# Ten split-operand buffers of a two-layer transformer kernel, set 32 to 224 bytes apart in SBUF

## The reference

```python
x = x + jnp.square(jax.nn.relu(hm @ w_up[l])) @ w_down[l]
...
hid = jax.nn.silu(xn @ w_gate[e]) * (xn @ w_up[e])
out = out + (hid * cw[..., e:e + 1]) @ w_down[e]
```

## Time and profile before

| | us |
|---|---|
| median of three runs | 964.89 |
| lowest and highest | 963.74, 967.37 |
| the profiled execution, its own time | 964.85 |
| its span, first to last instruction | 963.0 |
| TensorE busy | 947.5 |
| VectorE busy | 534.4 |
| ScalarE busy | 470.1 |

### The profile page before, as it was taken

The page is one execution under the profiler, slowest core; times in us unless marked ns, Lnnn a source line. Parts: engine busy times, 40 slices in busy tenths (PEclk is TensorE's granted clock), DMA queues, the critical chain, the costliest instruction groups (busy, mean ns, idle before and its releaser), DMA issues.

```text
span 963.0 us, 13218 instructions
## 1 busy us (share of the span) xinstructions
PE 947.5 (98%) x5313; PEld 722.7 (75%) x5313; DVE 534.4 (55%) x848; ACT 470.1 (49%) x733; POOL 2.5 (0%) x12
## 2 busy tenths in 40 slices
PE   9999999999999999999999999999999999999995
PEld 8878887887889998999889887889874354545432
DVE  5888896775666556555586874676453212122113
ACT  5488665756444444544566756445553121212113
POOL 0000000000000000000000000000000000000000
PEclk9999999999999999999999999999999999999999
DMA  9945465424455554554545725476858999999994
GB/s 314 303 143 173 155 238 179 156 107 163 152 189 190 204 175 175 175 181 156 202 150 175 246 104 175 131 259 223 290 205 286 393 394 393 394 393 395 393 396 157
DMA packets 107266, 223.49 MB, mean 232 GB/s; under 512 B 10186, under 2 KB 15043, under 8 KB 107203
## 3 DMA queue, kind: packets, MB, share of 16 engines
q1 hardware_dynamic: 104752, 219.10, 64.2%
q10 hardware_dynamic: 2450, 3.51, 1.1%
HBM read 221.54 MB, written 1.05 MB: 231 GB/s over the span
## 4 chain that ended last, share of the span: by engine, by line
PE 83%; DVE 7%; ACT 4%; issue 3%; DMA 2%; SPq 1%; POOL 0%; ACTq 0%; DVEq 0%; POOLq 0%
PE pb L477 17%; PE pb L479 17%; PE pb L478 17%; PE pb L2488 11%; PE pb L2511 5%; PE pb L2526 3%; PE pb L2455 2%; DVE wl L1552 2%; ACT wh L1003 2%; PE pb L567 2%; DMA BT<-in_w_exp_down 1%; PE pb L638 1%; DMA raw<-in_w_in 1%; PE pb L650 1%; PE pb L714 1%
## 5 line engine op out<-in xcount | busy, mean ns | idle before, releaser
L1552 DVE TENSOR_TENSOR wl<-raw,wh 128x2048 fp32r<-128x2048 f32 (+3 forms) x112 | 246.4, 2208 | 95.1 <-ACT wh L1003 94.8
L1003 ACT ACTIVATE wh<-raw 128x2048 fp32r<-128x2048 f32 (+3 forms) x112 | 206.7, 1852 | 108.6 <-PE pb L479 98.9
L477 PE MATMUL pb<-wh,th 128*128 128x512 f32 (+2 forms) x620 | 245.9, 397 | 0.2 <-DVE wl L1552 0.2
L479 PE MATMUL pb<-wh,tl 128*128 128x512 f32 (+2 forms) x620 | 239.0, 385 | 0.0
L478 PE MATMUL pb<-wl,th 128*128 128x512 f32 (+2 forms) x620 | 238.8, 385 | 0.0
L477 PE MATMUL pb<-th,wh 128*128 128x256 f32 x528 | 152.6, 289 | 0.0
L478 PE MATMUL pb<-tl,wh 128*128 128x256 f32 x528 | 149.4, 283 | 0.0
L479 PE MATMUL pb<-th,wl 128*128 128x256 f32 x528 | 149.4, 283 | 0.0
L477 PEld LDWEIGHTS pb<-wh,th 128*128 128x128 f32 x620 | 116.6, 188 | 26.1 <-issue 4.1
L479 PEld LDWEIGHTS pb<-wh,tl 128*128 128x128 f32 x620 | 116.4, 188 | 23.3
L478 PEld LDWEIGHTS pb<-wl,th 128*128 128x128 f32 x620 | 116.7, 188 | 20.4
(11 more groups left out here) (408 smaller groups left out, 1074.5 us busy)
## 6 DMA issues: line engine op xcount, KB each, us to landing
raw<-in_w_in SPq DMA_DIRECT2D x31, 1024.0 KB, 5.2
raw<-in_w_up SPq DMA_DIRECT2D x16, 1024.0 KB, 5.5
raw<-in_w_down SPq DMA_DIRECT2D x16, 1024.0 KB, 4.8
raw<-in_w_exp_gate SPq DMA_DIRECT2D x18, 512.0 KB, 11.2
raw<-in_w_exp_up SPq DMA_DIRECT2D x18, 512.0 KB, 11.9
raw<-in_w_xkv SPq DMA_DIRECT2D x8, 1024.0 KB, 5.1
raw<-in_w_exp_down SPq DMA_DIRECT2D x7, 1024.0 KB, 12.9
S<-in_w_exp_down SPq DMA_DIRECT2D x6, 1024.0 KB, 13.5
```

What stands on the lines that cost most here:

```text
L477: PE.matmul(o, lh, rh, start=start, stop=False, skip_group_check=True)
L479: return PE.matmul(o, ll, rh, start=False, stop=stop, skip_group_check=True)
L1003: ACTE.activation(hi_of(i), raw_of(i), ACT.Copy).then_inc(S["hi"], 1)
L1552: DVE.tensor_tensor(lo_of(i), raw_of(i), hi_of(i).bitcast(F), ALU.subtract).then_inc(S["lo"], 1)
```

## The change

Lines 193 to 196 get a small helper, `apart`, that declares an unused tensor of some fp32 columns ahead of a buffer. With 4 bytes a column the gaps are 32 bytes before tl0, wh0 and th1, 64 bytes before wh1, wh2, wl0, wl1 and wl2, 224 bytes before tl1, and none before th0. Sizes, names and uses of the buffers stay as they are, and the gaps are given back with the scope `early`.

```diff
--- before.py
+++ after.py
@@ -190,10 +190,19 @@
         RC = sb("RC", 2048)
         RDK = sb("RDK", 2048)
         RD, KT = RDK[:, 0:1024], RDK[:, 1024:2048]
-        TH, TL = [sbe("th0", 2048, R), 0], [sbe("tl0", 2048, R), 0]
-        WH = [sbe(f"wh{i}", SLOT, R) for i in range(NW)]
-        WL = [sbe(f"wl{i}", SLOT, R) for i in range(NW)]
-        TH[1], TL[1] = sbe("th1", 2048, R), sbe("tl1", 2048, R)
+        TH, TL, WH, WL = [0, 0], [0, 0], [0] * NW, [0] * NW
+
+        def apart(name, n, cols):
+            if cols:
+                sbe(f"gap_{name}", cols)
+            return sbe(name, n, R)
+
+        TH[0], TL[0] = apart("th0", 2048, 0), apart("tl0", 2048, 8)
+        for i in range(NW):
+            WH[i] = apart(f"wh{i}", SLOT, 8 if i == 0 else 16)
+        for i in range(NW):
+            WL[i] = apart(f"wl{i}", SLOT, 16)
+        TH[1], TL[1] = apart("th1", 2048, 8), apart("tl1", 2048, 56)
         BD = BT[:, 0:1024]
         TMP = BT[:, 1024:2304]
         PB = [ctx.enter_context(nc.psum_tensor(f"pb{i}", [128, 512], F)) for i in range(8)]
```

## The result

The changed kernel takes 969.25 us (median of 8 runs, 968.44 to 969.92) against 964.72 us of the kernel before in the same session (8 runs, 963.72 to 967.37). The ratio is 1.0045 with a 95% interval of 1.0034 to 1.0056: slower by 4.5 us. That is inside the 0.5% that I took as the least that can be told, but the interval leaves "no change" out, and the time lies above the range of 961 to 969. The profiled execution took 969.49 us, its span 967.6 us against 963.0.

A forecast was written before the change was run, and what follows sets the result against it. TensorE, busy 98% of the span, was taken to bound the kernel through the start-to-start time of three-pass matmuls. All terms were 0 us, summing to 0 against 964.85 us; forecast 964.9 us, range 961 to 969.

The forecast's parts named there:

- three-pass matmuls: 3,444 matmuls on lines 477 to 479: 0 us from moving their operands; range ends -13.3 and +7.5 ns each.
- The 288-column units: Line 477 at distances of 128, 256 and 384 bytes: 0.133 us per matmul at each, so distance gives nothing back.
- overhead of 13.3 ns: Width-independent remainder of each three-pass matmul; over 3,444 matmuls 45.9 us, the most the change could bring.
- The plain matmuls: Lines 541, 714 and 737, operands 0, 128 and 32 bytes apart: 0.216 us each, so distance gives nothing back.
- Line 2526: 512-column fp32r matmul, operands 160 bytes apart: 0.235 us, not less than 0.2275; distance gives nothing back.
- expert part: Stretch from 709.2 us on: same program at the same addresses, 0 us.
- B: Rival: new distances cost three-pass matmuls 7.5 ns each, 990.7 us, or 970 with one in five hit; chance 0.06.
- A: Rival: all 13.3 ns per three-pass matmul are same-distance collisions that end, 919.0 us, or 942 with half; chance 0.06.
- C: Rival: tl1 stays level with wh1, so if A holds those pairs keep their stall, 924 us; part of A's 0.06.
- The page's rule: Trainium skill page: loading the next tile's weights steals no read bandwidth from the running matmul; taken to speak against the change.
- ScalarE's and VectorE's splits: 112 splits on each engine, using the moved buffers: 0 us; at most 0.4 us per engine, covered by idle time.
- transfers: None writes the ten buffers while they are split operands; expert weights keep their addresses: 0 us.

The follow-up runs named there:

- e3: Kernel before the change, with only the low parts (TL and WL) moved by 64 bytes, high parts level; 966.99 us, ratio 1.0021.
- m2: TensorE-alone kernel in the three-pass order, distances in 16-byte steps (the three-pass map); 512 columns 226.7 to 227.3 ns at 0, 228.9 at 64.
- m1: TensorE-alone kernel, blocks of 24 fp32r matmuls, moving and stationary starts varied in 32-byte steps; blocks took 5.71 to 5.87 us (512 columns), 2.98 to 3.13 (256).
- e7: Kernel before, weight buffers 64 columns longer, only the stationary weights of 256-column units put 64 bytes into them; 961.07 us, ratio 0.9965.
- m4: TensorE-alone kernel, three passes, (moving, stationary) start pairs, four beginnings each, fixed or advancing tiles; (112, 0) ended at 113.3 ns for 256 columns.
- e2: Kernel before the change, with only the six weight buffers moved 64 bytes past the four activation buffers; 961.48 us, ratio 0.9969.
- e6: Kernel before the change, with only the weight buffers moved, 192 bytes from the activations; 969.06 us, ratio 1.0050.
- m3: TensorE-alone kernel, three passes, each distance begun six ways after plain matmuls of 128 to 188 columns; 256 columns at 64 bytes: 113.3 ns once, 117.8 five times.

## Why the prediction was wrong

*The step that failed* is the first term of the sum, three-pass matmuls, "I take 0 ns". The mean over the undisturbed steps was +4.3 ns for 512 columns and -1.2 ns for 256. The pace hangs on the distance between the operands, modulo 256 bytes; at equal distance, where the kernel before had all ten, 512 columns have their best pace and 256 columns nearly their worst (120.0 ns, of 120.3 at most). The change took both away from there.

On average the map gives this afterwards without a fitted number. Modulo 256 the change puts th0, tl0, th1, tl1 at 0, 32, 160, 128 past th0, wh0 to wh2 at 64, 128, 192 and wl0 to wl2 at 0, 64, 128. Over the 18 combinations of weight slot, activation slot and pass, the three-pass map's values for 512 columns average 232.0 ns; the trace of after has 232.1. For 256 columns, which use the first pair of activations alone, nine combinations average 117.3 ns with the fast rhythm at 64 and 192 throughout and 118.8 with the slow one; the trace has 118.6. That the average for 512 columns comes out to 0.1 ns is partly luck. Taken one by one the combinations do not follow the map, which was made with one distance at a time: wl0 with th0 and wh1 with tl1 are both at distance 0, 227.3 ns in the map, and step at 233.8 and 232.3 in the trace. Nor does it help to count the tile that is used next in place of the matmul's own: in e3 that distance is 0 for all three passes, and 512 columns step at 231.2. That the distances set the pace is shown; how a mixture of them adds up is not.

*The three tests in the trace of before.* Two were no tests and the third was discounted.
- The 288-column units: their distances of 0, 128, 256 and 384 bytes are 0, 128, 0, 128 modulo 256, two and not four, and at this width 128 bytes is worth 1.7 ns in m2, 0.005 us in the 0.40 us that I read to two decimals. I called this "the nearest" row because the code and buffers were the same; but the width was not that of the work, and the overhead of 13.3 ns that all widths share had made me treat widths as alike.
- The plain matmuls stood at 0.216 us with operands 0, 128 and 32 bytes apart. They say nothing of the three-pass ones, which load and move fp32r. Why plain ones don't react is open; no run here varied them.
- Line 2526 was the true signal. Its moving operand starts 160 bytes before the stationary one modulo 512, and so at 96 modulo 256, where both maps have 233.3 ns. The 0.235 us was one stretch; over all 90 undisturbed steps of the line the trace of before has 233.8 ns. The stretch reads the same in the changed kernel, whose expert part did not move, (851.58 - 850.17) / 6 = 0.235 us:

```profile
850.17 0.40 PE L2535 MATMUL pb<-YL,SET 128*128 128x512 f32 x1
...
851.58 0.40 PE L2535 MATMUL pb<-YL,SET 128*128 128x512 f32 x1
```

I set it aside for its bank changes and the 396 GB/s around it. m1 has neither and shows 233.3 ns at this distance against 226.7 to 227.3 at 0. The other excuse, that the first three 512-column matmuls in the earlier trace rows take 0.230 us at equal distance, looks like the settling: in m1's block at distance 0 the steps after the first take 224 to 236 ns, 231.8 on average over nine, and the last ones 226.7.

*The rivals.* B, "the new distances cost", had the right mechanism and the right point of decision (0.229 us for 512 columns; it came to 0.232). Its price was too high: 7.5 ns is what the worse distances of the map cost (its worst is 236.8 ns, at 240 bytes), the average of this change's is 4.3, and it was applied to 256 columns too, where the sign is the other. With B's own price of 7.5 on 512 columns alone it would have read 964.9 + 1,728 x 7.5 ns = 977.9 us. A, "collisions end", is right in sign for 256 columns alone: the most that any distance gave back there is 6.7 of the 13.3 ns, and none gave 512 columns anything. C, tl1 level with wh1, is there in the addresses but can't be told in the trace (232.3 ns for that pair, 231.8 and 232.8 for tl1 with the other two slots).

*The page's rule.* By the Trainium skill, page "TensorE: Matmul & The Clock Gate", section "Step-by-step: what each phase is for", loading the next tile's weights does not steal read bandwidth from the running matmul. I took that to speak against any effect. m1 shows one all the same: with TensorE alone at work, the placement of the stationary tile against the moving one is worth up to 7.6 ns of 227 and 6.7 of 120. Whether it is read bandwidth that is lost there, no run shows. The same page's figure for isolated matmuls, 216 and 109 ns by "Back-to-back issue gap", was not reached by three-pass matmuls at any distance tried.

*What held.* ScalarE's and VectorE's splits, transfers and the expert part were put at 0 and came to 0: 1913 and 2289 ns, and no drift from 714 to 927 us. So did the reading that TensorE's busy time is the time: all that the change did went into the span, nothing was covered. *The range* was too tight by its own evidence: with +7.5 ns kept as an end and 1,728 matmuls of 512 columns, half of that price is already +6.5 us. Giving B no more than 0.06 was the error behind it.

*Left open:* which part of the memory or of TensorE makes the pattern; whether the stationary tile that counts is that of the running matmul or the one loaded for the next, or whether both do; and whether 113.3 ns can be had in every 256-column unit, which would be worth at most 1,557 x 3.1 ns = 4.8 us more than e7. The pairs that always ended at 113.3 in m4, (112, 0), (144, 32) and (208, 16), need activations at starts that the 512-column units also use; that was not tried in the kernel.

## What to carry to other kernels

When a TensorE-bound kernel pairs streaming fp32r tiles with freshly loaded ones, look at their starts modulo 256 bytes for each width: level was best for 512 columns and nearly worst for 256, so spreading buffers evenly can cost (here 0.45%) where one chosen distance gains (weights 64 bytes past activations, -0.3%). Measure the pace over distance with a small kernel of TensorE alone at the real widths before arguing from neighbours. At one distance for all it gave the pace of this kernel to about 1 ns for 512 columns (228.9 for 229.6 in e2, 233.3 for 233.3 in e6); for 256 columns it gave the two rhythms, but not which one a unit takes, and for a mixture of distances it was right only on average. So try the placement in the kernel as well. And a row that differs from the work in two harmless-looking respects, like line 2526, is a bound to be priced and not a thing to be explained away, while a row of the same code at another width may be no bound at all.

## What the runs showed of the hardware that I had not expected

- A pace that depends on the starts of both operands with a period of 256 bytes: 226.7 to 237 ns for 512 columns of fp32r, 113.3 to 120.3 for 256, 131.7 to 133.4 for 288, 173.3 to 176 for 384.
- Settling: a run of equal matmuls begins with some nine steps of 224 to 236 ns and only then falls to 226.7 ns (m1, 512 columns, distance 0); at (112, 0) a block of 256 columns takes up to 14 steps, all but the first of 114 to 123 ns, before it falls to 113.3 (m4).
- Two stable rhythms at one distance, 113.3 and 117.8 ns at 64 and at 192 bytes, picked by how the run begins (m3) and, once settled, not left until it ends (e2, 117.8 ns for up to 167 steps).
- A mixture of distances that costs more than either one: 232.0 ns with the low moving part at 64 bytes and the rest at 0, against 228.9 and 227.3 (m2, 512 columns).
- A stationary operand that starts on an odd multiple of 16 bytes behaves as if it were at another distance: (0, 144) 116.7 to 120.0 ns, where (112, 0), the same difference, ends at 113.3 (m4).
